# Feed-forward up weights as seven half-size products in place of eight

## The reference, cut to what matters

```python
h = rmsnorm(x, norm2_g[l])
u = h @ w_ffn_up[l]                     # 1024 x 5632
a, b = u[..., :D_FF], u[..., D_FF:]     # D_FF = 2816 = 22 tiles of 128
a = causal_dwconv(a, ffn_conv_w[l], ffn_conv_b[l])   # 3 taps along the sequence
x = x + (jax.nn.silu(a) * b) @ w_ffn_down[l]
```

## Time and profile before

| | us |
|---|---|
| three runs | 3500.39, 3500.40, 3500.96, median 3500.4 |
| the profiled execution, first to last instruction (span) | 3506.0 |
| busy TensorE, share of the span | 3359.6, 96% |
| busy VectorE | 1864.9, 53% |
| busy GpSimd | 1206.0, 34% |
| busy ScalarE | 788.7, 22% |

### The profile page before, as it was taken

One profiled execution on the slowest core, in us unless ns is written; L12 is line 12 of the kernel. 1 busy time (PEld: TensorE's weight loads), 2 busy tenths in 40 slices (PEclk: granted clock), 3 DMA queues, 4 the chain that ended last, 5 costly groups with the idle time before them and its releaser, 6 DMA issues.

```text
span 3506.0 us, 54999 instructions
## 1 busy us (share of the span) xinstructions
PE 3359.6 (96%) x22562; PEld 2695.1 (77%) x22562; DVE 1864.9 (53%) x2499; ACT 788.7 (22%) x1284; POOL 1206.0 (34%) x571
## 2 busy tenths in 40 slices
PE   7999788999999999989999999999989999999997
PEld 6878678688888888867777678888867677688886
DVE  7445644546676676765544454433646544543433
ACT  4222344221101101133223320000333332300001
POOL 3323344134444444432222234444322222244444
PEclk9999899999999999999999999999999999999998
DMA  3121100311111111131121121111321111211111
GB/s 138 37 94 43 49 4 4 130 48 49 48 48 48 48 48 48 42 122 49 43 54 49 42 84 49 48 48 48 111 66 43 48 42 49 79 48 49 48 48 66
DMA packets 62333, 198.00 MB, mean 56 GB/s; under 512 B 10736, under 2 KB 21712, under 8 KB 60256
## 3 DMA queue, kind: packets, MB, share of 16 engines
q1 hardware_dynamic: 44832, 140.05, 11.9%
q10 hardware_dynamic: 17344, 55.63, 4.9%
HBM read 167.16 MB, written 16.96 MB: 53 GB/s over the span
## 4 chain that ended last, share of the span: by engine, by line
PE 90%; DVE 6%; ACT 2%; issue 1%; POOL 1%; DMA 1%; ACTq 0%; POOLq 0%; DVEq 0%; SPq 0%
PE ps L555 56%; PE ps L1066 10%; PE ps L1448 5%; PE ps L1230 3%; PE ps L1257 3%; PE ps L1275 3%; DVE sc L2890 2%; PE ps L865 1%; PE ps L841 1%; PE ps L1184 1%; PE ps L1094 1%; PE ps L933 0%; ACT GB L1752 0%; PE ps L810 0%; PE ps L743 0%
## 5 line engine op out<-in xcount | busy, mean ns | idle before, releaser
L445 POOL TENSOR_TENSOR wH<-wraw,pv 128x1024 fp32r<-128x1024 f32 x239 | 464.7, 1944 | 2103.1 <-PE ps L555 1708.2
L555 PE MATMUL ps<-hH,wH 128*128 128x512 f32 x2800 | 879.0, 395 | 26.1 <-DVE hL L2345 11.5
L555 PE MATMUL ps<-hL,wH 128*128 128x512 f32 x2800 | 871.6, 393 | 0.0
L555 PE MATMUL ps<-hH,wL 128*128 128x512 f32 x2800 | 870.6, 392 | 0.0
L447 POOL TENSOR_TENSOR wL<-wraw,wH 128x1024 fp32r<-128x1024 f32 x239 | 624.3, 2612 | 18.8
L555 PEld LDWEIGHTS ps<-hH,wH 128*128 128x128 f32 x2800 | 521.6, 189 | 139.6 <-issue 18.0
L555 PEld LDWEIGHTS ps<-hL,wH 128*128 128x128 f32 x2800 | 524.6, 189 | 110.6 <-issue 1.7
L555 PEld LDWEIGHTS ps<-hH,wL 128*128 128x128 f32 x2800 | 524.8, 189 | 109.1 <-issue 0.3
L2672 DVE TENSOR_TENSOR xT<-ps,xT 128x512 f32<-128x512 f32 x544 | 361.7, 689 | 6.6 <-PE ps L1094 6.6
L2993 DVE TENSOR_TENSOR sg<-ps,mrows 128x1024 f32<-128x1024 f32 x46 | 56.3, 1225 | 359.9 <-PE ps L555 359.9
L1986 ACT ACTIVATE sc<-sc,stat 128x256 f32<-128x256 f32 (+7 forms) x256 | 171.1, 669 | 126.7 <-DVE stat L2897 65.1
(11 more groups left out here) (445 smaller groups left out, 4275.5 us busy)
## 6 DMA issues: line engine op xcount, KB each, us to landing
wraw<-ws SPq DMA_DIRECT2D x242, 512.0 KB, 3.3
park<-xT ACTq DMA_DIRECT2D x2, 4096.0 KB, 13.4
xT<-park ACTq DMA_DIRECT2D x2, 4096.0 KB, 12.4
recT<-out ACTq DMA_DIRECT2D x28, 256.0 KB, 3.9
xT<-xin SPq DMA_DIRECT2D x4, 1024.0 KB, 8.9
xT<-xin ACTq DMA_DIRECT2D x1, 4096.0 KB, 12.4
sc<-kraw ACTq DMA_DIRECT2D x32, 128.0 KB, 2.3
out<-xT SPq DMA_DIRECT2D x16, 256.0 KB, 2.1
```

The lines of the kernel that those rows point to most:

```text
L445: pool.tensor_tensor(wH[:, j, :], wraw[:, j, :], zero, ALU.add).then_inc(w_hi, 1)
L555: mm = pe.matmul(pair(p)[:, half * HALF:(half + 1) * HALF], wp, hp[:, k, half * HALF:(half + 1) * HALF], start=(m == 0 and n == 0), stop=( ...
```

## The change

The two up slots of a tile (a and b) and the two halves of the sequence are seen as a matrix of 2 x 2 blocks: weights W11, W12 (a, first and last four feature blocks) and W21, W22 (b), activations of the first and last four feature blocks by the first and second half of the sequence. The product of two such matrices takes eight block products (of 4 feature blocks x 3 passes = 12 matmuls each); here it is made of seven, by sums and differences of blocks.

- **Tile 0** is done as before, by two `col_gemm`. The tiles 1 to 21 are done by `up_pair`: seven products P0 to P6 of 12 matmuls, into the PSUM banks A, E, A, B, A, C, A. Between them partial sums are moved from bank to bank: ScalarE copies A to B after P0 (`seed`), and E to SBUF after P1 (`shared_product`); VectorE adds A and that into C after P2 (`up_seed`). P2, P4 and P6 wait for these.
- **Weights.** GpSimd makes four sums of half a slot for each tile, and splits seven units of 128 x 512 (`unit_low`: an addition of zero, a subtraction) into a ring of four buffers in the half of `hH` and `hL` that nothing else reads any more. The down slot is split as before, but into the one buffer j = 1, so that its split waits for the end of the down product before it. SP loads halves of slots in an order of its own.
- **Activations.** Four sums of blocks are made once, ahead of the loop (`mix_sums`, `mix_rest` on VectorE, `mix_weighted` on ScalarE), rounded by ScalarE (`mix_hi`), and their low parts are made by GpSimd (two) and VectorE (two).
- **Order.** TensorE now does for each tile f: up pair of f, down of f-1. VectorE: convolution of f-1, `ffn_scale` (b times `frows`, both in SBUF), `up_seed`, gate (both factors in SBUF), low part, three exits of 512 out of PSUM (`up_exits`), then the row additions. The gate itself no longer reads PSUM.
- The loop is written out for four tiles and runs five times; tile 21 stands behind it. The buffers `apad`, `aconv`, `frows`, `gH`, `gL` lie elsewhere. Semaphores of the first stage are used again with an offset (`since`).
- Slot numbers of the layers behind shift (`USE_LAYER`, `BACK`), and the split of the first two layer slots waits for the down products' own semaphore.

The core of the diff:

```diff
+            def unit_low(f, q, u):
+                s = ring_at(q, u)
+                src = (upA[:, 0, :], unit_sum[s][:, :], upA[:, 0, :], upA[:, 1, :], upB[:, 0, :], unit_sum[s][:, :],
+                       upB[:, 1, :])[u]
...
+                pool.tensor_tensor(unit_hi[s][:, :], src, zero_half, ALU.add).then_inc(sem("up_hi"), 1)
+                pool.wait_ge(sem("up_hi"), since("up_hi", f * UNITS + (u + 1 - UNITS)))
+                pool.tensor_tensor(unit_lo[s][:, :], src, unit_hi[s][:, :], ALU.subtract).then_inc(sem("up_lo"), 1)
+
+            def first_units(f, q):
...
+                unit_low(f, q, 0)
+                pool.wait_ge(sem("up_A21"), since("up_A21", f * 16))
+                pool.wait_ge(sem("up_A22"), since("up_A22", f * 16))
...
+                pool.tensor_tensor(s1[:, :], upB[:, 0, :], upB[:, 1, :], ALU.add).then_inc(sem("up_sum"), 1)
...
+                pool.tensor_tensor(upB[:, 0, :], upA[:, 0, :], upB[:, 0, :], ALU.subtract).then_inc(sem("up_sum"), 1)
...
+                pool.tensor_tensor(upA[:, 0, :], s1[:, :], upA[:, 0, :], ALU.subtract).then_inc(sem("up_sum"), 1)
+                unit_low(f, q, 1)
+                unit_low(f, q, 2)
+                unit_low(f, q, 3)
+
+            def later_units(f, q):
+                unit_low(f, q, 4)
+                pool.wait_ge(sem("up_used"), since("up_used", f * UNITS - 1))
+                pool.tensor_tensor(unit_sum[ring_at(q, 5)][:, :], upA[:, 1, :], upA[:, 0, :], ALU.subtract
+                                   ).then_inc(sem("up_sum"), 1)
+                unit_low(f, q, 5)
+                unit_low(f, q, 6)
+
+            def down_split(f):
+                pool.wait_ge(sem("down_raw"), since("down_raw", f * 16))
+                pool.wait_ge(sem("down_done"), since("down_done", f))
+                pool.tensor_tensor(wH[:, 1, :], wraw[:, 1, :], zero, ALU.add).then_inc(sem("down_hi"), 1)
+                pool.wait_ge(sem("down_hi"), since("down_hi", f))
+                pool.tensor_tensor(wL[:, 1, :], wraw[:, 1, :], wH[:, 1, :], ALU.subtract).then_inc(sem("down_ready"), 1)
...
+                for q in range(LOOP_TILES):
+                    f = i * LOOP_TILES + (q + 1)
+                    down_split(f)
+                    later_units(f, q)
+                    first_units(f + 1, q + 1)
...
+            def up_pair(f, q):
...
+                pe.wait_ge(sem("a_free"), since("a_free", f))
+                product(0, A_BANK, True)
+                pe.wait_ge(sem("e_copied"), since("e_copied", f))
+                pe.wait_ge(sem("row_added"), f * KT - 2)
+                product(1, E_BANK, True)
+                pe.wait_ge(sem("b_seeded"), since("b_seeded", f))
+                product(2, A_BANK)
+                product(3, B_BANK)
+                pe.wait_ge(sem("c_seeded"), since("c_seeded", f))
+                product(4, A_BANK)
+                product(5, C_BANK)
+                pe.wait_ge(sem("ae_added"), since("ae_added", f + 1))
+                product(6, A_BANK)
...
-                ffn_up(0, u, g * 2, "ff_a")
-                ffn_down(1, u, g * 2 - 2, 0)
-                ffn_down(0, u + 1, g * 2 - 1, 1)
-                ffn_up(1, u + 1, g * 2, "ff_g")
-                ffn_up(0, u + 2, g * 2 + 1, "ff_a")
-                ffn_up(1, u + 2, g * 2 + 1, "ff_g")
+                for q in range(LOOP_TILES):
+                    up_pair(i * LOOP_TILES + (q + 1), q)
+                    ffn_down(i * LOOP_TILES + q)
```

ScalarE ahead of the loop:

```diff
+            mix_weighted()
+            mix_hi(0, 1)
+            mix_hi(1, 2)
             act.wait_ge(sem("mean_ready"), 2)
...
+            mix_hi(3, 3)
+            mix_hi(2, 4)
             act.wait_ge(sem("rstd_rows"), 2)
             act.activation(frows[:, :], pair(2), ACT.Copy).then_inc(sem("rows_ready"), 1)
```

VectorE ahead of the loop and in it:

```diff
+            mix_sums()
             dve.wait_ge(sem("rms_ready"), 2)
...
+            mix_rest()
             dve.wait_ge(sem("rows_ready"), 1)
...
+                    ffn_conv(f - 1)
+                    ffn_scale(f - 1)
+                    up_seed(f)
+                    ffn_gate(f - 1)
+                    ffn_low(f - 1, gH[:, :], gL[:, :])
+                    up_exits(f)
+                    row_add(f * KT - KT, f - 1, (sem("down_done"), since("down_done", f + 1)), pairs=(2, 3, 1))
```

More of the change, by code:

```diff
@@ L425, in _ @@
                 last = start + LAYER_SLOTS - 6
-                slots(start, [start + n for n in (1, 4, 2, 3, 5, 0)])
-                weights(start + 6, last)
-                slots(last, [last + n for n in (0, 2, 3, 4, 1, 5)])
+                order = [start + n for n in (1, 4, 2, 3, 5, 0)]
+                if L == 0:
+                    sp.dma_start(wraw[:, 0, :], ws[order[0]]).then_inc(raw_full[0], 16)
+                    sp.wait_ge(sem("last_ready"), since("last_ready", 1))
+                    sp.dma_start(wraw[:, 1, :], ws[order[1]]).then_inc(raw_full[1], 16)
+                    slots(start + 2, order[2:], BACK)
+                else:
+                    slots(start, order, BACK)
+                weights(start + 6, last, back=BACK)
+                slots(last, [last + n for n in (0, 2, 3, 4, 1, 5)], BACK)
             for h in range(2):
@@ new lines, in _ @@
+            for n in range(2):
+                pool.wait_ge(sem("mix_hi"), since("mix_hi", n + 1))
+                pool.wait_ge(sem("mix_sum"), since("mix_sum", n + 2))
+                pool.tensor_tensor(mixL[n][:, :, :], mixS[n][:, :, :], mixH[n][:, :, :], ALU.subtract).then_inc(sem("mix_lo"), 1)
+            first_units(1, 0)
+            pool.wait_ge(gemm_done[1], USE_LAYER)
+            with pool.Fori(0, (FFN_ROWS - 1) // LOOP_TILES) as i:
+                for q in range(LOOP_TILES):
[3 more added lines that the diff above has]
+                    first_units(f + 1, q + 1)
@@ L1071, in row_gemm, with product @@
                     mm.then_inc(sem("row_done") if e < KT - 1 else gemm_done[j], 1)
[L1073 to L1078, removed]
+            def up_pair(f, q):
+                first = f * UNITS - UNITS
+                halves_of = ((hH, hL, 0, 0), (hH, hL, 4, 0), (hH, hL, 4, HALF))
+                def product(u, b, start=False):
+                    x = UNIT_OF[u]
+                    if x < 3:
+                        hi, lo, k0, c0 = halves_of[x]
+                    else:
+                        hi, lo, k0, c0 = mixH[x - 3], mixL[x - 3], 0, 0
+                        pe.wait_ge(sem("mix_lo"), since("mix_lo", x - 2))
+                    s = ring_at(q, u)
+                    pe.wait_ge(sem("up_lo"), since("up_lo", first + (u + 1)))
+                    for k in range(4):
+                        w = [r[s][:, k * P:(k + 1) * P] for r in (unit_hi, unit_lo)]
+                        for n, (wp, xp) in enumerate(((w[0], hi), (w[0], lo), (w[1], hi))):
+                            mm = pe.matmul(bank(b), wp, xp[:, k0 + k, c0:c0 + HALF], start=(start and k == 0 and n == 0),
+                                           stop=(k == 3 and n == 2), skip_group_check=True)
+                    mm.then_inc(sem("up_used"), 1)
+                pe.wait_ge(sem("a_free"), since("a_free", f))
[11 more added lines that the diff above has]
+                product(6, A_BANK)
@@ L1080, in last_rows @@
+            def last_rows(ready, n, pairs, parts, lo, free, rows, done):
                 for group in range(2):
@@ L1082, in last_rows @@
                         if group == 0:
-                            pe.wait_ge(w_ready[j], use + 1)
+                            pe.wait_ge(*ready[j])
                             pe.wait_ge(sem("row_lo"), lo + j)
-                        hi, low = parts[j]
+                        (hi, low), (wh, wl) = parts[j], rows[j]
                         for q in range(4):
@@ new lines, in first_half, with up_period @@
+            def first_half(f):
+                act.wait_ge(sem("up_used"), since("up_used", f * UNITS + RING))
+                act.wait_ge(sem("ff_g"), f)
+                act.activation(braw[:, 0:HALF], bank(A_BANK), ACT.Copy).then_inc(sem("a_free"), 1)
+            def up_period(f, q, hi, last=False):
+                seed(f)
+                ffn_silu(f - 1)
+                shared_product(f)
+                if not last:
+                    act.wait_ge(sem("down_done"), since("down_done", f))
+                ffn_hi(f - 1, hi)
+                first_tap(f)
+                first_half(f)
@@ L2704, in _ @@
             own.wait(dve)
[L2705 removed]
+            for name in ("ae_added", "row_lo", "down_done"):
                 dve.sem_inc(sem(name), 1)
@@ L2738, in layer_input @@
+            f = FFN_ROWS
+            ffn_conv(f - 1)
+            ffn_scale(f - 1)
+            up_seed(f)
+            ffn_gate(f - 1)
+            ffn_low(f - 1, gH2[:, 0, :], gL2[:, 0, :])
+            up_exits(f)
+            ffn_conv(f)
+            ffn_scale(f)
+            ffn_gate(f)
+            ffn_low(f, gH2[:, 1, :], gL2[:, 1, :])
```

(1 more changed line is left out.)

373 lines of the change are left out of this document (273 added, 100 removed).

## The result

| | before | after |
|---|---|---|
| median of 5 runs each, us | 3501.0 (3500.4 to 3503.5) | 3517.9 (3514.1 to 3520.2) |
| ratio, 95% interval | | 1.0042 (1.0029 to 1.0054) |
| profiled execution's span, us | 3506.0 | 3512.8 |
| GpSimd busy | | 1574.8 us, 45% |

In a second set of runs (experiment 5) the changed kernel gave 3515.8 and a ratio of 1.0035 (1.0021 to 1.0048). The forecast was 3510, in a range of 3484 to 3534.

A forecast was written before the change was run, and what follows sets the result against it. TensorE bounds the kernel before, GpSimd after: -57.1 + 41.2 + 11.7 + 6.7 + 2.0 + 2.1 + 3.0 = +9.6, taking the profiled execution from 3506.0 to 3515.6 and the median to 3510 us, range 3484 to 3534.

The forecast's parts named there:

- P0 of tile 1: Ahead of the loop: VectorE's differences and GpSimd's low parts delay tile 1's first product to 803.5, +11.7 us in all.
- first period: Tile 1: two more 2048-column VectorE differences delay `up_seed` to 15.7; period 36.7, +6.7 us, with +2 for the clock.
- exit: Behind the loop: tile 21's pair ends later, +2.1 us, and the last downs wait for its low part, +3.0.
- The bound and the turns: In the loop: GpSimd becomes the bound, as five VectorE turns add 4.65 to its 27.0 us, making 31.7 a tile.
- The first rival: In the loop: VectorE's turns cost GpSimd nothing, TensorE stays the bound at 30.03 a tile; time 3465, chance 0.15.
- the two on GpSimd's price: In the loop: GpSimd is the bound but cheaper, 3490 to 3503, or dearer, 3520 to 3535; chance 0.2 each.
- One sign: In the loop's trace: VectorE's taps, scale, gate and low part would last 1.5 to 2.4 if the forecast was right.
- The chain through the units: In each tile: down, split, unit 4, sum, unit 5, P5, P6, down, together 32.15 us.
- each of the eight waits for one GpSimd instruction: Ahead of the loop: `mix_rest`'s eight VectorE instructions take turns with GpSimd one by one, from 782 to 799.
- the second rival: GpSimd is the bound but cheaper, or turns ahead of the loop are fewer: 3490 to 3503, chance 0.2.
- From trace to median: Whole kernel: the runs' median lies 0.2% under the profiled execution, so 3515.6 becomes 3510.
- the clock in the loop: TensorE waits 2.2 ahead of P5 each tile; if its clock fell, time would end in the range's upper third.

The follow-up runs named there:

- experiment 5: The changed kernel again with no edit, on the chip of four further runs, against the kernel before: 3515.8 us, ratio 1.0035.
- experiment 1: Changed kernel with taps, scale, gate and low part reading a quiet PSUM pair, so VectorE takes no turns: 3467.2 us, ratio 0.9902 to the kernel before.
- experiment 2: Changed kernel with only `ffn_scale` reading a quiet PSUM pair, one turn fewer: 3488.1 us, ratio 0.996 to the kernel before.
- experiment 6: Changed kernel with the seven roundings of a tile's units moved from GpSimd to ScalarE: 3470.9 us, ratio 0.991 to the kernel before.
- experiment 4: Changed kernel with units 4 to 6 split ahead of the down's slot: 3486.1 us, ratio 0.9953 to the kernel before.
- experiment 7: Changed kernel with factor rows and tile 0's exits put before `mix_rest` ahead of the loop: 3516.7 us, ratio 1.0035 to the kernel before.
- experiment 9: experiment 7 plus GpSimd's order ahead of the loop changed, unit 0, sums and unit 1 before the second low part: 3514.4 us, ratio 1.003 to the kernel before.
- experiment 10: Changed kernel with the next layer's first split held back until the last low part is made: 3516.0 us, ratio 1.0034 to the kernel before.
- experiment 3: Changed kernel with GpSimd making the sum ahead of unit 5 twice in each tile: 3579.4 us, ratio 1.0221 to the kernel before.

## Why the prediction was right, and where it was not

| step | predicted | measured |
|---|---|---|
| short addition, subtraction | 1.04, 1.28 | 1.04, 1.28 |
| GpSimd's tile without turns or load | 27.0 | 26.4 |
| five turns | 4.65 | 4.70 |
| wait for the half load | 0.35 | 0.63 |
| period | 32.2 | 32.04 |
| loop, 19 periods over 30.03 | +41.2 | +38.1 |
| factor rows; P0 of tile 1 in all | +1.9; +11.7 | +1.8; +8.5 |
| first period, clock with it | +6.7, +2.0 | +12.5 |
| from P0 of tile 21 to the gates | +2.1, +3.0 | +9.6 |
| sum with -57.1 | +9.6 | +11.6 |

Read directly, the stretch from `gsum` to the gates grew by 11.3 (719.2 to 730.4), and by 12.1 in experiment 5. The medians grew by 16.9 and 13.3. What the difference is made of beyond the stretch stays open: the work ahead of it is the same, yet `gsum` comes anywhere between 762.8 and 772.0 in the thirteen traces.

The sum is better than its terms. The loop was forecast 3.1 too dear and P0 of tile 1 by 3.2, the first period 3.8 too cheap and the exit 4.5; that these nearly cancel is luck.

- *The bound and the turns.* Right, and shown by experiments 1, 2 and 6: take the turns or the work from GpSimd and the period is TensorE's 30.03. The first rival (turns that cost nothing) and the two on GpSimd's price fell with the 1.04 and the 4.70. GpSimd's tile is 0.6 shorter than forecast: I gave 0.04 to each of eight gaps where nothing is waited for, and in the trace the next instruction starts 0.04 ahead of the end of the one before. One sign was too narrow: the five VectorE instructions take 1.23 to 3.18, not 1.5 to 2.4.
- *The chain through the units.* Right: it ends last by 0.4, as experiment 2 (without it) and 4 (its order) show.
- *P0 of tile 1.* The step "each of the eight waits for one GpSimd instruction" failed for the first four, so this part is 3.2 less than forecast, which the second rival had as a possibility ("the turns ahead of the loop are fewer"). I had missed that GpSimd's second low part itself waits for them. The step missed as well that GpSimd's queue is a second chain of the same length, so that moving VectorE's work alone gives nothing (experiments 7 and 9).
- *First period.* The term was too small by 3.8. I had P4 wait for `up_seed`, 15.7 behind P0 (that gives a period of 34.9, with three products and the down; how 36.7 was reached is not shown). It waits for unit 4 instead, and comes 21.7 behind: GpSimd pays some 2 for a turn with a difference of 2048 columns (1.9 and 2.05), and the prediction gave such a turn no price of its own. This wait of 5.4 also brings a second spell of the lower clock.
- *Exit.* The term was too small by 4.5. I costed tile 21's taps and scale at 1.2 each, with GpSimd at rest; it starts the layer's split there, and experiment 10 takes 3.7 of it back.
- *From trace to median.* I carried over that the profiled execution lay 0.2% above the median. After, it lay 0.1% below. So this step took 5.6 off where 5.1 had to be added: 10.7, more than the whole change of 9.6, and the largest error of the forecast. The 3510 is 7.9 too low because the span had been put 2.8 too high (3515.6 for 3512.8). The profiled execution of before had spent 6.1 more ahead of the feed-forward part, and nothing said that the next one would.

The forecast left the clock in the loop alone, with a wait of 2.2 ahead of P5. The clock did stay, but at a wait of 1.7; no run has 2.2, 2.8 brings it down once at the exit and 3.1 in the loop, so there was less room than I knew.

## What to carry to other kernels

When work is moved to an idle engine, lay out that engine's whole queue for one period, with the price of each turn that another engine takes, before counting what TensorE saves: here 57 us of products cost 17 in one layout and gained 43 in another. Take from the newly bound engine first the instructions that a third engine can do without turns (here the roundings), and put ahead in its queue what the next product waits for. At both ends of such a stretch, read the queues of all engines together: removing one wait showed the next, twice.

## Not expected of the hardware

- The clock can fall behind a single short wait. It stayed at 1.00 behind 1.7 us in each 32, and fell to 0.60 behind 2.8 (experiment 10) and to 0.50 and 0.59 behind 3.1 (experiment 3: 888 to 892, 924 to 928). In experiment 3 a tile grew by 3.2 for 1.4 of work; that the other 1.8 are the clock's is read from these windows, not tested by itself.
- What a turn costs GpSimd follows the length of VectorE's instruction, not of its own: 0.84 to 1.04 beside 1.2 (1024 columns), with GpSimd's at 512 or 1024; 1.9 and 2.05 beside some 2.3 (2048 columns); 0.31 to 0.46 beside some 0.65 (512 columns; units of 1.50, 1.59 and 1.71 in place of 1.04, 1.28 and 1.29). About 0.3 less than VectorE's own duration, in all three. The Trainium skill (SBUF — State Buffer, "Who interferes with whom") calls the port pair that the two engines share "an exclusive lock", so that one waits while the other's instruction holds it. The three sizes agree with that but for the 0.3.
